# Recurrences in chunks: two chunks substituted and merged at a time

## The reference, cut to what matters

```python
def first_block(x, ...):
    for l in range(DEPTH):                     # DEPTH = 2
        x = x + 0.5 * swiglu(...)
        ya = dsa_attention(pa, ...)
        yb, v_first = rwkv7_time_mix(pb, ...)  # S = S*w + (S a) b^T + v k^T ; y = S r
        yc = gated_deltanet(pc, ...)           # per chunk, below
        x = x + concatenate([ya, yb, yc]) @ w_out[l]
        x = x + 0.5 * swiglu(...)

def chunk_gated_delta_rule(q, k, v, g, beta):
    lower = where(strict, (kb @ k^T) * decay, 0)
    sol = triangular_solve(eye(C) + lower, rhs, lower=True, unit_diagonal=True)
    u, wk = sol[..., :Dv], sol[..., Dv:]
    intra = where(incl, (q @ k^T) * decay, 0)
    def step(S, inp):                          # one after the other over the chunks
        v_new = uc - wc @ S
        o = (qc * exp(gc)) @ S + ac @ v_new
        S = S * exp(g_last) + (kc * exp(g_last - gc))^T @ v_new
        return S, o
```

## Time and profile before

| | |
|---|---|
| median of three runs | 3484.43 us |
| profiled execution, its own time | 3478.72 us |
| its span in the trace | 3476.9 us |
| TensorE busy | 3358.7 us, 97% of the span |
| VectorE busy | 1424.3 us, 41% |
| ScalarE busy | 1267.1 us, 36% |
| GpSimd busy | 1675.9 us, 48% |

### The profile page before, as it was taken

The page is one execution under the profiler, slowest core; times in us unless marked ns, Lnnn a source line. Parts: engine busy times, 40 slices in busy tenths (PEclk is TensorE's granted clock), DMA queues, the critical chain, the costliest instruction groups (busy, mean ns, idle before and its releaser), DMA issues.

```text
span 3476.9 us, 47334 instructions
## 1 busy us (share of the span) xinstructions
PE 3358.7 (97%) x16932; PEld 2760.2 (79%) x16932; DVE 1424.3 (41%) x2739; ACT 1267.1 (36%) x1976; POOL 1675.9 (48%) x2052
## 2 busy tenths in 40 slices
PE   7999998899999999999989999999899999999999
PEld 6888776788888888887668888878667888888887
DVE  5431598855221322148786522123663110441100
ACT  4222436534222322234563422232533332433321
POOL 6765542006665566655400466645304555435554
PEclk9999999799999999999979999999999999999999
DMA  5443321003443344333100344332102222212222
GB/s 186 145 145 109 109 91 56 13 19 133 145 144 110 127 145 145 121 103 98 61 25 1 109 145 145 127 104 82 58 1 91 97 97 97 85 61 97 97 97 97
DMA packets 104225, 340.51 MB, mean 98 GB/s; under 512 B 12144, under 2 KB 17936, under 8 KB 103968
## 3 DMA queue, kind: packets, MB, share of 16 engines
q1 hardware_dynamic: 87824, 283.08, 24.6%
q10 hardware_dynamic: 16272, 55.65, 4.8%
HBM read 330.78 MB, written 2.65 MB: 96 GB/s over the span
## 4 chain that ended last, share of the span: by engine, by line
issue 38%; POOL 33%; PE 27%; DVE 1%; POOLq 0%; ACT 0%; DVEq 0%
POOL w_lo L721 33%; PE ps L2313 7%; PE ps L2314 7%; PE ps L2315 7%; PE ps L3094 1%; PE ps L2336 0%; PE ps L3073 0%; PE ps L2337 0%; PE ps L2341 0%; PE ps L3082 0%; PE ps L3184 0%; DVE stat L2214 0%; DVE sq L2207 0%; PE ps L3190 0%; PE ps L3074 0%
## 5 line engine op out<-in xcount | busy, mean ns | idle before, releaser
L721 POOL TENSOR_TENSOR w_lo<-w_raw,w_hi 128x256 fp32r<-128x256 f32 x2040 | 1669.2, 850 | 1783.3 <-ACT w_hi L764 1776.1
L2313 PE MATMUL ps<-h_hi,w_hi 128*128 128x512 f32 x2608 | 1019.9, 391 | 0.9 <-ACT mem L981 0.9
L2315 PE MATMUL ps<-h_hi,w_lo 128*128 128x512 f32 x2608 | 1015.7, 389 | 0.0
L2314 PE MATMUL ps<-h_lo,w_hi 128*128 128x512 f32 x2608 | 1015.6, 389 | 0.0
L764 ACT ACTIVATE w_hi<-w_raw 128x1024 fp32r<-128x1024 f32 x510 | 538.2, 1057 | 927.2 <-DMA w_raw<-in_tiles 927.0
L2313 PEld LDWEIGHTS ps<-h_hi,w_hi 128*128 128x128 f32 x2608 | 490.0, 188 | 113.3 <-issue 6.4
L2315 PEld LDWEIGHTS ps<-h_hi,w_lo 128*128 128x128 f32 x2608 | 490.0, 188 | 102.9
L2314 PEld LDWEIGHTS ps<-h_lo,w_hi 128*128 128x128 f32 x2608 | 490.0, 188 | 100.3
L2314 PE MATMUL ps<-a_lo,w_hi 128*128 (+1 forms) x1120 | 435.8, 389 | 0.0
L2313 PE MATMUL ps<-a_hi,w_hi 128*128 (+1 forms) x1056 | 410.8, 389 | 0.0
L2315 PE MATMUL ps<-a_hi,w_lo 128*128 (+1 forms) x1056 | 410.8, 389 | 0.0
(11 more groups left out here) (477 smaller groups left out, 3589.4 us busy)
## 6 DMA issues: line engine op xcount, KB each, us to landing
w_raw<-in_tiles SPq DMA_DIRECT2D x510, 512.0 KB, 3.3
ada_raw<-in_ada_tiles ACTq DMA_DIRECT2D x96, 512.0 KB, 3.3
mem<-mem SPq DMA_DIRECT2D x80, 64.0 KB, 2.1
x<-in_x_t SPq DMA_DIRECT2D x2, 1024.0 KB, 6.6
sq<-in_cond ACTq DMA_DIRECT2D x4, 512.0 KB, 4.2
mem<-gates SPq DMA_DIRECT2D x8, 256.0 KB, 3.9
consts<-in_consts SPq DMA_DIRECT2D x1, 1280.0 KB, 12.8
core_mem<-gates SPq DMA_DIRECT2D x8, 128.0 KB, 2.9
```

What stands on the lines that cost most here:

```text
L721: ins = nc.gpsimd.tensor_tensor(w_lo[:, s, part], w_raw[:, s, part], w_hi[:, s, part].bitcast(F32), ALU.subtract)
L2313: nc.tensor.matmul(bank, wh, hi, start=first, stop=False, skip_group_check=True)
L2314: nc.tensor.matmul(bank, wh, lo, start=False, stop=False, skip_group_check=True)
L2315: return nc.tensor.matmul(bank, wl, hi, start=False, stop=last, skip_group_check=True)
```

## The change

VectorE substitutes two chunks at once: the tiles are 16 blocks wide (8 heads x 2 chunks), so the steps have 128x16 to 128x240 columns. There are two substitutions in a layer instead of four. The merges of both chunks of a pair go together. At level 4 TensorE makes lower products of 64 columns only and one set of inverse products; the product is masked behind it, by VectorE (`mask_products`), and the transposed inverse comes by a VectorE transpose. `lower_corners` and the constant `levels` are gone. The order is now one function `core` for each engine. ScalarE copies eight of the ten turned operands out ahead of the last two decays and the table load. The state has two buffers, an even and an odd chunk have grams and banks of their own.

```diff
@@ VectorE @@
                 for t in steps:
                     w = 16 - t
-                    row, product = (... [:, 0:8 * w] ... h=8 ...)
+                    row, product = (... [:, 0:16 * w] ... h=16 ...)
                     link(V.stream_shuffle(row, C_Y16[:, :, t:16], ...))
-                    link(V.tensor_tensor(product, row, C_M16[:, :, t:t + 1].to_broadcast([P, 8, w]), ALU.mult))
+                    link(V.tensor_tensor(product, row, C_M16[:, :, t:t + 1].to_broadcast([P, 16, w]), ALU.mult))
                     link(V.tensor_tensor(C_Y16[:, :, t:16], C_Y16[:, :, t:16], product, ALU.add))
+                def mask_products(n):
+                    for g in range(2):
+                        dve.wait_ge(S["t1_ready"], merge_turn(TB * l + n, 4, g) + 1)
+                        V.tensor_tensor(out, src, own_pair, ALU.mult).then_inc(S["t1_out"], 1)
+                def merge16(n):
+                    for g in range(2):
+                        dve.wait_ge(S["dx_ready"], merge_turn(TB * l + n, 4, g) + 1)
+                        link(V.tensor_tensor(evens(inv, 4), evens(inv, 4), compact(ps[...], 4), ALU.add))
+                        V.transpose(inv_t, inv).then_inc(S["merged16"], 1)
+                substitute(range(15, 0, -1))
+                spread_inverses(l, 0)
+                fresh_rows()
+                mask_products(0)
+                mask_products(1)
+                take_a_grams(0, (0, 1))
+                merge16(0)
+                V.tensor_tensor(mem[:, 37:39, :], ...)
+                V.scalar_tensor_tensor(mem[:, 24:26, :], ...).then_inc(S["gdn_ready"], 1)
+                merge16(1)
+                take_grams(l, 2)
+                small_blocks(l, 2)
+                take_a_grams(0, (2, 3))
+                take_grams(l, 3)
+                small_blocks(l, 3)
+                substitute(range(15, 0, -1))
+                take_a_grams(1, (0, 1))
+                next_state(1)
+                spread_inverses(l, 2)
+                take_a_grams(1, (2, 3))
+                next_state(2)
+                mask_products(2)
+                mask_products(3)
+                merge16(2)
+                take_a_grams(2, range(4))
+                merge16(3)
+                take_a_grams(3, (0, 1))
+                next_state(3)
+                take_a_grams(3, (2, 3))
@@ TensorE @@
+                a_grams(0, (0, 1))
+                for even in (0, 2):
+                    odd, n = even + 1, even + 1
+                    lower_products(even, 4)
+                    lower_products(odd, 4)
+                    inverse_products(even, 4)
+                    inverse_products(odd, 4)
+                    if even:
+                        a_grams(even, (0, 1))
+                    else:
+                        lower_grams(l, 2)
+                    lower_products(even, 5)
+                    lower_products(odd, 5)
+                    inverse_products(even, 5)
+                    inverse_products(odd, 5)
+                    if even == 0:
+                        lower_grams(l, 3)
+                    lower_products(even, 6)
+                    inverse_products(even, 6)
+                    right_sides(n)
+                    lower_products(odd, 6)
+                    writes(n)
+                    a_grams(odd, (0,))
+                    inverse_products(odd, 6)
+                    state_products(n)
+                    outputs(n)
+                    a_grams(odd, (1,))
+                    right_sides(n + 1)
+                    writes(n + 1)
+                    state_products(n + 1)
+                    outputs(n + 1)
@@ ScalarE @@
                 for n in range(2):
                     decays(n).then_inc(S["eg_ready"], 1)
+                for u in (2, 3, 4, 5, 0, 1):
+                    turn_out(mem[:, u, :])
+                for c, u in enumerate((45, 6)):
+                    turn_out_scaled(mem[:, u, :], c, ST_DELTA)
                 decays(2)
                 decays(3).then_inc(S["eg_ready"], 1)
                 load_silu()
-                for u in (2, 3, 4, 5, 0, 1):
-                    turn_out(mem[:, u, :])
-                for c, u in enumerate((45, 6)):
-                    turn_out_scaled(mem[:, u, :], c, ST_DELTA)
                 for c, u in enumerate((26, 19)):
                     turn_out_scaled(mem[:, u, :], c, ST_BETA)
```

More of the change, by code:

```diff
@@ L598, in _ @@
         def _(sp):
-            first, last = 2 * P, CONST_AT["eps"]
+            first, last, small = 2 * P, CONST_AT["sel_pair"], CONST_AT["eps"]
             half = KD // 2
@@ L2762, in inverse_products, with lower_products @@
-                def inverse_products(lev, g):
-                    pe.wait_ge(S["t1_out"], merge_turn(b, lev, g) + 1)
+                slot = lambda ru, hh, j: ru[:, P * j + HD * hh:P * j + HD * hh + HD]
+                def lower_products(n, lev):
+                    b = TB * l + n
+                    for g in range(2):
+                        pe.wait_ge(S[{4: "small_ready", 5: "merged16", 6: "merged32"}[lev]], 2 * b + g + 1)
+                        first = {4: 0, 5: 32, 6: HD}[lev]
+                        rows = slice(HD, P) if lev == 6 else slice(0, P - first)
+                        for h in range(4):
+                            inv = inv_units(n)[:, g, blk(h)]
+                            out = ps[rows, merge_bank(n, g), HD * h:HD * h + HD]
+                            ins = nc.tensor.matmul(compact(out, lev), lower_units(n)[:, g, P * h + first:P * h + P], evens(inv, lev), start=True, stop=True)
+                        ins.then_inc(S["t1_ready"], 1)
@@ L2774, in inverse_products @@
-                    for h in range(4):
-                        rows = slice(0, P if lev == 4 else HD)
-                        out = compact(ps[rows, 4 + g, HALF + HD * h:HALF + HD * h + HD], lev)
-                        ins = nc.tensor.matmul(out, t1(h), odds(inv_t(h), lev), start=True, stop=True)
-                    ins.then_inc(S["dx_ready"], 1)
-                def a_grams():
-                    if b > 1:
-                        pe.wait_ge(S["y_out"], b - 1)
-                    if n == TB:
-                        return
-                    if n + 1 < TB:
-                        pe.wait_ge(S["gram_taken"], 2 * b + 4)
-                    elif n > 1:
-                        pe.wait_ge(S["s_out"], b)
-                    grams((0, 1), "a_gram_ready", ((kt, ap), (kt, rt)), last)
-                    if n > 1:
-                        grams((6, 7), "a_gram_ready", ((nb, rt), (kg, qg)), last)
@@ L2793, in right_sides @@
-                def right_sides():
+                    for g in range(2):
+                        pe.wait_ge(S["t1_out"], merge_turn(b, lev, g) + 1)
+                        bank = merge_bank(n, g)
+                        inv_t = lambda h: inv_t_units(n)[:, g, blk(h)]
+                        t1 = lambda h: t1_of(n, g)[:, HD * h:HD * h + HD]
+                        if lev < 6:
+                            first = 0 if lev == 4 else 32
+                            for h in range(4):
+                                ins = nc.tensor.matmul(ps[0:P - first, bank, HD * h:HD * h + HD], inv_t(h)[:, first:P], t1(h), start=True, stop=True)
+                        if lev > 4:
+                            for h in range(4):
+                                out = compact(ps[0:HD, bank, HALF + HD * h:HALF + HD * h + HD], lev)
+                                ins = nc.tensor.matmul(out, t1(h), odds(inv_t(h), lev), start=True, stop=True)
+                        ins.then_inc(S["dx_ready"], 1)
@@ L2795, in right_sides, with a_grams @@
+                def a_grams(n, kinds):
+                    for kind in kinds:
+                        pairs = ((kt, ap), (kt, rt)) if kind == 0 else ((nb, rt), (kg, qg))
+                        grams([a_banks(n, 2 * kind + hh) for hh in range(2)], "a_gram_ready", pairs, n)
+                def right_sides(n):
+                    b, last = TB * l + n, n - 1
                     if n == 1:
@@ L2839, in outputs @@
+                def outputs(n):
+                    b, last = TB * l + n, n - 1
+                    tm = lambda u, hh: mem[:, u, last * P + HD * hh:last * P + HD * hh + HD]
+                    pe.wait_ge(S["a_gram_out"], 4 * b)
+                    if n > 1:
+                        pe.wait_ge(S["y_out"], b - 1)
+                    for c in range(2):
+                        nc.tensor.matmul(ps[:, 7, blk(c)], state_of(n)[:, c, :], rt(c)[:, blk(last)], start=True, stop=False)
                         for hh in range(2):
@@ L2840, in outputs @@
                             rows = slice(HD * hh, HD * hh + HD)
[L2841 to L2842 removed]
+                            nc.tensor.matmul(ps[rows, 7, blk(c)], tm(v_t[c], hh), a_grams_of(last, hh)[:, blk(2 + c)], start=False, stop=False)
                         for hh in range(2):
                             rows = slice(HD * hh, HD * hh + HD)
[L2845 removed]
```

(2 more changed lines are left out.)

383 lines of the change are left out of this document (161 added, 222 removed).

## The result

The changed kernel takes 3511.36 us (median of nine executions, 3499.26 to 3524.80), the kernel before 3484.18 (nine, 3479.33 to 3488.19). The ratio is 1.0078, 95% interval 1.0059 to 1.0096: 27 us slower. The forecast was 3500, slower, in a range of 3474 to 3513; the result is 2 us inside its upper end. The profiled execution took 3506.78, its span is 3504.7.

A forecast was written before the change was run, and what follows sets the result against it. TensorE, busy 97%, was taken as the bound, so VectorE savings count only where it waits. Schedule -3.2 plus low clocks 6.3 and 4.8 gave +7.9 us a layer, +15.8 in all: median 3500, range 3474 to 3513.

The forecast's parts named there:

- the forecast's own: Range 3493 to 3508 for two low-clock stretches, substitution 1 us either way, half or all of the stretches; chance 0.40.
- rival B: Recurrences: the third stretch, level 5 of the second pair, is low too; +14.2 us a layer, 3513; chance 0.15.
- the third low stretch: Level 5 of the second pair, after a 2.5 us wait: low clock costing 0 to 6.3 us, taken as 0.
- the sum: Both recurrences: -3.2 for the schedule, +6.3 and +4.8 for low clocks, +7.9 us a layer, +15.8 for two.
- VectorE's prices: Wider substitution: 45 instructions take 14.6 us by the column slope; transpose 0.7; VectorE saves 9.7 us a pair.
- Level 4 and the start: Layer 0: ScalarE's last copies end 651.3, first grams 654.9, level 4 of both chunks 663.3.
- The first low stretch: TensorE over 665 to 682, after grams, level 4 and a wait: clock falls, +6.3 us a layer.
- rival A: Clock stays high from 655: -3.2 us a layer, 3478, or 3472 with first grams high too; chance 0.20.
- The wait for the state: TensorE ends chunk 1's outputs at 690.7 and waits 6.0 us for the first state update, done at 696.6.
- The outputs: Chunk 1's level 6, right sides, writes and outputs end at 690.7; later, level 6 and steps 3 and 4 take 23.8.
- One output bank with its wait: Outputs in one bank: costed at nothing, since the copy is out 6 us earlier.
- the second low stretch: Behind the wait for the state: state products, step 2 outputs, two level-4 groups at half speed; +4.8, bounds 0 and 4.8.

The follow-up runs named there:

- the mended order: Changed kernel with outputs grouped by kind in two banks, two VectorE merges moved earlier, chunk 3's grams ahead of level-5 inverses, chunk 2's output grams between inverses: 3475.1 us.
- the first experiment: Changed kernel with chunk 1's output-gram maskings and the first state update moved ahead of the second substitution's last four steps: 3503.2 us, 1.0083.
- the filled wait: Changed kernel with four unused 128x512 products added in TensorE's wait for the first state: 3510.1 us, 1.0080.
- the grouped outputs: Changed kernel with the outputs' products grouped by kind in two banks, not alternating in one: 3512.8 us, 1.0078.
- the wide level 4: Changed kernel with level-4 lower products of 128 moving columns again, not 64: 3507.1 us, 1.0067.
- chunk 2's output grams left ahead: The mended order, but chunk 2's output grams stay ahead of the second pair's level-5 lower products: 3478.1 us, 0.9979.
- the mixed level 5: Changed kernel with two unused 128x512 products added in each pair, one ahead of each chunk's level-5 inverse products: 3507.0 us, 1.0073.
- gram early and outputs grouped: Changed kernel with chunk 3's grams between the level-5 inverses of chunks 0 and 1, and outputs grouped in two banks: 3490.9 us, 1.0027.

## Why the prediction was right, and where it was off

**Sign and mechanism held, the size only just.** The loss is the late chunk-3 gram, the state update behind the whole second substitution, and low clocks on a path that is now TensorE's. Putting the late gram back into the mended order moved the median by 8.2 us and the spread from 8 to 34. The median of 3511.4 lies outside the forecast's own 3493 to 3508 and 2 us from rival B's 3513: the third low stretch, which B had and the sum did not, came in both layers of the profiled execution. That the sum was no further off owes something to luck, since two other errors of 3 us a layer cancelled.

**VectorE's prices held.** The first substitution was forecast for 635.9 to 650.5 and ran 635.91 to 650.78. A 128x240 instruction starts 0.46 after the one before (649.40 to 649.86), forecast 0.43; the 128x512 transpose took 0.71, forecast 0.7. The slope over a width without a row was good for 2%.

**Level 4 and the start were cheaper.** ScalarE's last turned operand was out at 649.15, forecast 651.3, so the first grams started 2.1 us earlier, and level 4 took 7.3 and not 8.4. Together 3 us in hand at 660.29.

**The first low stretch held**: forecast 665 to 682, found 665 to 678. It is not a matter of the program alone: the same instructions ran at 1.00 in another execution, so the profiled one could also have gone rival A's way here.

**The wait for the state** was 4.43 and not 6.0, under the 5 to 7 that would have shown the forecast right, since TensorE came late to it. From the start of chunk 3's gram to the wait TensorE took 19.3 us (675.50 to 694.8), forecast 16.4 (674.3 to 690.7): 1.1 more in the outputs, the rest mainly in the gram and the level-6 products behind it, at the low clock until 679.

**The outputs** are one of the two terms of the sum that were mis-sized: "level 6, right sides, writes and outputs of chunk 1", and the outputs of the later chunks, used those of before, 2.4, where they take 3.48. "One output bank with its wait" was costed at nothing, and the turns that its order brings were not counted. The six turns more than before make 1.0 at 0.17 each, four times a layer; one of the four only shortens the wait. That is 3 us a layer, 6 in all. Taken back alone in the mended order they cost 5.3 (3480.4 against 3475.1), with overlapping intervals.

**The third low stretch** is the other mis-sized term: it was priced at 0, bounds 0 to 6.3. It came in layer 0 (728 to 737, at 0.50): the inverse halves took 9.5 us (727.95 to 737.4), not 5.4. That is +4.1. It came in layer 1 too (1893 to 1905, at 0.50). The step that failed is the reason given, that the 2.60 wait of before had dropped nothing. The wait here was shorter, 1.50 (726.06), and the clock fell all the same, over a run of small products.

**The sum for layer 0.** Forecast +7.9, found +10.6: 7.9 - 3.0 (start and level 4) + 3.1 (outputs) + 4.1 (third stretch) make 12.1. Of the 1.5 over, 1.1 is the second low stretch, which cost 3.7 and not 4.8: it slowed the right sides (699.23 to the writes at 704.52, 5.3 us; 3.2 at the high clock in the first experiment, 696.45 to 699.64), the state products (2.7 against 1.4) and the first of the outputs (0.3), and was over before the level-4 groups that had been priced. In layer 1 it was +14.5: the start took 1.5 us longer, and the clock was low again over its last outputs (from 1927 on), which took 6.0 and not 3.6.

So the two recurrences came to +25.1 where the sum had +15.8, and 2.7 us more lie outside them. How much of the 27 us between the medians is clock can be estimated only: the nine executions of after fit 2429 us for each unit of mean clock, so 0.0086 under before is 21 us, and 6 is left for work and waits. The fit is a correlation inside one kernel, carried a little beyond its range, and longer waits and low clocks come together, so I don't call this split shown.

**Rival A** had 3472 to 3478, with the clock high throughout. The mended order runs at 3475, but it does not test A: its order is another, its outputs are cheaper, and its clock was low over 1799 to 1826.

**Two rules of the Trainium skill.** Narrowing the lower products saved 0.006 us a record, so the isolated gap of the Trainium skill (TensorE: Matmul & The Clock Gate, section Back-to-back issue gap) does not price them; that section's remark on the weight load does. The single figure of the Trainium skill's section LDWEIGHTS, same page, would make a low stretch free if the load alone paced the small products; level-5 inverse halves took 1.35 at the high clock and 2.52 at the low, and the measurement decides.

**What stays open.** What exactly takes the clock down in an unmixed level-5 run was not found. With the waits ahead of it filled, three runs of four still fell; with products mixed in, four of four mostly kept the clock; and yet unmixed runs stood at 1.00 in several profiles: the first run of layer 0 with the filled wait, the grouped outputs and the wide level 4, and the second of both layers with chunk 2's output grams left ahead. Nor was it found why, in seven of the twelve edited kernels' profiles, the clock of layer 1 stayed at 0.50 for 23 us or more around level 4 and the first level-5 run (1811 to 1847 with the filled wait, 1799 to 1826 in the mended order). In these seven layer 1 took 5 to 21 us longer than layer 0, and neither the forecast nor an expectation has such a stretch.

## What to carry to other kernels

A merged step saves its own engine time, and then the inputs of its second half decide: move what the long step waits for ahead of work that can wait, and only then judge the merge. What a new wait of TensorE costs cannot be read from its length: with the gram late, one program took from 3472 us, no more than without the wait, to 3506. So look at the spread and the mean clock of the executions as well as at the median. When a bank is saved by another order of products, count the turns between 128-wide and 64-wide ones.

## What the runs showed of the hardware

- Turning between products whose output takes 128 array columns and ones that take 64 costs about 0.17 us a turn at the high clock, in the mean: outputs of 32 records took 3.48 us with seven turns, 2.80 with three, about 2.4 with one.
- The same instructions, in two executions, ran at a granted clock of 1.00 and of 0.59 over the same dozen microseconds (664 to 676, the filled wait and after).
- Ten waits of TensorE for the state were longer than 4 us (4.43 to 6.06: after, the grouped outputs, the mixed level 5, the wide level 4 and the late gram, both layers of each). The clock of the 12 us or so behind was 0.50 to 0.68 in all ten. Behind waits of 1.4 and 1.6 us it was 0.86 to 1.00, and 0.86 too where there was no such wait (the state update inside the substitution). At 2.70 and 2.39 (gram early and outputs grouped) it was 0.50 in one layer and 0.86 in the other, and at 2.60 in before 1.00.
- Over the 4 us behind the wait for ScalarE ahead of the ninth turned operand, 7.6 to 8.0 us long, the clock was 0.50 in both layers of every profile in which that wait was not filled, after included.
